# Moving per-head statistics of a recurrent layer's output from VectorE to ScalarE, and reordering the solve around it

## What is computed

```python
_, y = lax.scan(_rwkv7_step, S0, seq)                 # y: tokens x 16 heads x 64
mean = jnp.mean(y, axis=-1, keepdims=True)
var = jnp.mean(jnp.square(y - mean), axis=-1, keepdims=True)
yn = ((y - mean) * lax.rsqrt(var + LNX_EPS)).reshape(B, T, D) * lnx_w + lnx_b
bonus = (jnp.sum(rh * kh * r_k, axis=-1, keepdims=True) * vh).reshape(B, T, D)
out = ((yn + bonus) * g).astype(x.dtype)
return out @ w_o
```

## Time and profile before

| what | us |
|---|---|
| median of three runs | 1098.86 |
| the three runs | 1093.63, 1098.86, 1102.5 |
| the profiled execution, its own time | 1091.18 |
| its span | 1089.3 |

### The profile page before, as it was taken

The page is one execution under the profiler, slowest core; times in us unless marked ns, Lnnn a source line. Parts: engine busy times, 40 slices in busy tenths (PEclk is TensorE's granted clock), DMA queues, the critical chain, the costliest instruction groups (busy, mean ns, idle before and its releaser), DMA issues.

```text
span 1089.3 us, 18693 instructions
## 1 busy us (share of the span) xinstructions
PE 1062.2 (98%) x7143; PEld 917.0 (84%) x7143; DVE 798.9 (73%) x1103; ACT 604.0 (55%) x928; POOL 219.3 (20%) x234
## 2 busy tenths in 40 slices
PE   7999998999999999999999999999999999999997
PEld 6997797888888888789888888998777789888886
DVE  7997878778886658777788756688867776666643
ACT  6766363555564566856666554635665446555532
POOL 0125493121221011002222200571100001122200
PEclk9999999999999999999999999999999999999999
DMA  8553172646666466345667575556452555766552
GB/s 249 172 172 117 39 244 69 175 135 181 187 192 253 167 151 162 121 131 150 187 189 192 194 271 158 159 191 215 154 136 84 194 162 131 193 191 193 193 193 78
DMA packets 219747, 183.11 MB, mean 168 GB/s; under 512 B 43265, under 2 KB 197614, under 8 KB 219678
## 3 DMA queue, kind: packets, MB, share of 16 engines
q1 hardware_dynamic: 215710, 171.43, 52.4%
q0 software_dynamic: 3392, 8.66, 2.5%
q10 hardware_dynamic: 576, 2.07, 0.5%
HBM read 179.44 MB, written 2.69 MB: 167 GB/s over the span
## 4 chain that ended last, share of the span: by engine, by line
PE 80%; DVE 13%; issue 2%; DMA 2%; ACT 1%; POOL 1%; SPq 1%; DVEq 0%; POOLq 0%; ACTq 0%
PE bank L288 20%; PE bank L282 13%; PE bank L284 13%; PE bank L283 13%; PE bank L289 10%; DVE ring L417 3%; PE bank L295 2%; PE bank L1250 2%; DVE arena L1687 1%; DVE arena L1782 1%; DVE stat L1780 1%; PE bank L375 1%; PE bank L2167 1%; DMA arena<-in_kv_w_up 1%; PE bank L1365 1%
## 5 line engine op out<-in xcount | busy, mean ns | idle before, releaser
L417 DVE TENSOR_TENSOR ring<-ring,arena 128x2048 fp32r<-128x2048 f32 (+1 forms) x138 | 312.9, 2271 | 112.4 <-ACT arena L411 110.8
L282 PE MATMUL bank<-arena 128*128 128x512 f32 (+3 forms) x980 | 343.6, 351 | 3.7 <-DVE ring L417 3.0
L288 PE MATMUL bank<-arena 128*128 128x512 f32 x960 | 335.7, 396 | 0.0
L411 ACT ACTIVATE arena<-ring 128x2048 fp32r<-128x2048 f32 (+1 forms) x145 | 272.1, 1879 | 98.0 <-DMA ring<-in_ffn_w_out 42.9
L289 PE MATMUL bank<-arena,ring 128*128 128x256 f32 x960 | 267.2, 278 | 0.0
L284 PE MATMUL bank<-arena 128*128 128x512 f32 (+3 forms) x720 | 264.7, 368 | 0.0
L283 PE MATMUL bank<-ring,arena 128*128 128x512 f32 (+2 forms) x560 | 216.1, 386 | 0.0
L288 PEld LDWEIGHTS bank<-arena 128*128 128x128 f32 x960 | 180.1, 188 | 42.6
L282 PEld LDWEIGHTS bank<-arena 128*128 128x128 f32 x980 | 185.4, 189 | 29.2 <-issue 5.4
L289 PEld LDWEIGHTS bank<-arena,ring 128*128 128x128 f32 x960 | 180.6, 188 | 0.0
L284 PEld LDWEIGHTS bank<-arena 128*128 128x128 f32 x720 | 135.6, 188 | 22.2
(11 more groups left out here) (338 smaller groups left out, 1274.9 us busy)
## 6 DMA issues: line engine op xcount, KB each, us to landing
ring<-in_ffn_w_in SPq DMA_DIRECT2D x80, 512.0 KB, 5.1
ring<-in_ffn_w_out SPq DMA_DIRECT2D x44, 512.0 KB, 4.4
ring<-in_w_gate_up SPq DMA_DIRECT2D x40, 512.0 KB, 5.1
ring<-in_w_in SPq DMA_DIRECT2D x18, 1024.0 KB, 5.1
ring<-in_a_w_rkv SPq DMA_DIRECT2D x12, 1024.0 KB, 5.4
ring<-in_w_down SPq DMA_DIRECT2D x22, 512.0 KB, 3.7
ring<-in_a_w_o SPq DMA_DIRECT2D x4, 1024.0 KB, 6.8
arena<-in_ffn_w_in SPq DMA_DIRECT2D x8, 512.0 KB, 4.7
```

The source lines that it names most:

```text
L282: nc.tensor.matmul(dst, stationary[0], moving[0], start=start, stop=False)
L288: nc.tensor.matmul(dst[:, :], stationary[0], both_parts, start=start, stop=False)
L411: nc.scalar.activation(buf(hi_of(n), 0, w, arena12), ring[:, r, 0:w], ACT.Copy).then_inc(hi_ready, 1)
L417: on.tensor_tensor(ring12[:, r, 0:w], ring[:, r, 0:w], buf(hi_of(n), 0, w, arena12).bitcast(F32), ALU.subtract).then_inc(split_ready, 1)
```

## The change

Seven edits in the lists of four engines:

1. **Statistics on ScalarE.** The 128x32 scaling of the value means, and the four 128x8 scalings of sums to variances, become ScalarE copies with a scale (and a bias). The two sums of values become one over both tiles.
2. **The root's product on ScalarE.** `scaled(a, q)`: eight ScalarE copies of 128x64 out of the bank, each scaled by its head's root, instead of L1811 on VectorE. `gated_out` keeps two instructions.
3. **VectorE's order in the solve.** All block additions of tile 1 come ahead of `gated_out(0, 0)`. The first sum of squares comes ahead of `state_added`.
4. **GpSimd's second centring held** until VectorE's split of the first `w_o` slot is done.
5. **ScalarE's order.** The split of `w_o` slot 1 moves up behind the first squares; `scaled(0, *)` stands ahead of the split of the last `w_o` slot; `scaled(1, *)` behind the early rounded part.
6. **TensorE's order.** Both block inverses of tile 1 ahead of `o_turn(0, 0)`; `o_turn(1, 1)` ahead of (1, 0).
7. **VectorE's order behind the solve.** Both last `w_o` splits ahead of `gated_out(1, *)`. `early_lo(0, 0)` moves from between `o_lo(1, 0)` and `o_lo(1, 1)` to the place of `early_lo(0, 1)`, and that one behind `turn_dve` of tile 0.

```diff
 # ffn_front_dve
             x_scaled(dve, i + 1, 0, xn)
             if f != 1:
-                early_lo(dve, f, 1)
-            turn_dve(dve, turn, 0, 4, hi, lo)
+                early_lo(dve, f, 0 if f == 0 else 1)
+            turn_dve(dve, turn, 0, 4, hi, lo)
+            if f == 0:
+                early_lo(dve, f, 1)
             post_scale(dve, i, 1)
 # rwkv_pe
             block_inverses(1, 0)
+            block_inverses(1, 1)
             o_turn(0, 0)
-            block_inverses(1, 1)
             for q in range(2):
-                pe.wait_ge(u_out, 2 + q + 1)
+                pe.wait_ge(solve_out, 4 + q + 1)
                 y_solved(1, q)
...
                 elif (a, s) == (1, 0):
+                    o_turn(1, 1)
                     pe.wait_ge(o_split, 3)
-                elif (a, s) == (1, 1):
-                    o_turn(1, 1)
 # rwkv_act
             def squares(a, q):
                 act.wait_ge(ymm, 2 * a + q + 1)
-                if a == 1:
-                    act.wait_ge(var_ready, 2 + q + 1)
+            def variance(a, q):
+                stat = slice(a * H + 8 * q, a * H + 8 * (q + 1))
+                act.wait_ge(stats_ready, 2 + 2 * a + q + 1)
+                nc.scalar.activation(y_var[:, stat], y_sq[:, stat], ACT.Copy, bias=LNX_EPS, scale=1.0 / N).then_inc(var_ready, 1)
+            def scaled(a, q):
+                act.wait_ge(rstd_ready, 2 + 2 * a + q + 1)
+                for h in range(8 * q, 8 * q + 8):
+                    op = nc.scalar.activation(toks(W_YC)[:, a, h * N:(h + 1) * N], bank[Y_BANK[a][q]][:, h % 8 * N:(h % 8 + 1) * N],
+                                              ACT.Copy, scale=y_rstd[:, a * H + h:a * H + h + 1])
+                op.then_inc(solve_out, 1)
...
+            act.wait_ge(stats_ready, 1)
+            nc.scalar.activation(v_mean, v_sum, ACT.Copy, scale=-1.0 / N).then_inc(stats_ready, 1)
             for b in range(4):
                 step_evac(b)
...
             squares(0, 0)
+            act.wait_ge(state_mm, 1)
+            ahead(act, FIRST["w_o"] + 1, split_act)
+            variance(0, 0)
             squares(0, 1)
+            variance(0, 1)
             ahead(act, FIRST["w_o"] + 2, split_act)
+            scaled(0, 0)
+            scaled(0, 1)
             act.wait_ge(sweep_mm, SOLVED + SWEEP_NO[1, 2])
             ahead(act, LAST["w_o"], split_act)
             solutions(1, 0)
             solutions(1, 1)
             o_evac(0, 0)
             squares(1, 0)
+            squares(1, 1)
             o_evac(0, 1)
-            squares(1, 1)
+            variance(1, 0)
+            variance(1, 1)
             early_hi(act, 0, 0)
+            scaled(1, 0)
+            scaled(1, 1)
             o_evac(1, 0)
             o_evac(1, 1)
 # rwkv_dve
-                nc.vector.tensor_scalar(y_var[:, stat], y_sq[:, stat], 1.0 / N, LNX_EPS, ALU.mult, ALU.add).then_inc(var_ready, 1)
...
-                dve.wait_ge(rstd_ready, 2 + 2 * a + q + 1)
-                link(dve, nc.vector.tensor_tensor(by_head(yc), by_head(bank[Y_BANK[a][q]][:, :]), spread(y_rstd[:, stat].unsqueeze(2), [P, 8, N]), ALU.mult))
+                dve.wait_ge(solve_out, 4 * a + 2 + q + 1)
...
-            for a in range(NT):
-                value_means(a)
+            nc.vector.tensor_reduce(v_sum, by_head(buf(W_V)), AX, ALU.add).then_inc(stats_ready, 1)
...
+            squares_summed(0, 0)
             state_added(0)
             state_added(1)
-            variance(0, 0)
+            squares_summed(0, 1)
             block_added(1, 0, 1)
-            variance(0, 1)
             block_added(1, 0, 2)
             block_added(1, 1, 1)
-            gated_out(0, 0)
             block_added(1, 0, 3)
             block_added(1, 1, 2)
             block_added(1, 1, 3)
+            gated_out(0, 0)
             gated_out(0, 1)
             o_lo(0, 0)
             ahead(dve, FIRST["w_o"] + 1, split_dve)
-            variance(1, 0)
+            squares_summed(1, 0)
             o_lo(0, 1)
-            variance(1, 1)
+            squares_summed(1, 1)
             ahead(dve, FIRST["w_o"] + 2, split_dve)
+            ahead(dve, LAST["w_o"], split_dve)
             gated_out(1, 0)
-            ahead(dve, LAST["w_o"], split_dve)
             gated_out(1, 1)
             o_lo(1, 0)
-            early_lo(dve, 0, 0)
             o_lo(1, 1)
 # rwkv_pool
             rest_gated(0)
+            pool.wait_ge(split_ready, SPLIT_NO[FIRST["w_o"]] + 1)
             values_centred(1)
             rest_gated(1)
```

More of the change, by code:

```diff
@@ L1118, in build @@
         (n_saved, nd_landed, solved, y_saved, z_zeroed, z_landed, cleared, tok_mm, tok_evac, u_mm, u_rhs, step_mm, step_in,
-         sweep_mm, sum_ready, u_out, rem_mm, state_mm, state_ready, ymm, lnx_landed, means_ready, s1_zeroed, c_ready,
+         sweep_mm, sum_ready, solve_out, rem_mm, state_mm, state_ready, ymm, lnx_landed, stats_ready, s1_zeroed, c_ready,
          o_ready, o_mm, o_in, o_split) = (
             sem(n) for n in ("n_saved", "nd_landed", "solved", "y_saved", "z_zeroed", "z_landed", "cleared", "tok_mm",
-                             "tok_evac", "u_mm", "u_rhs", "step_mm", "step_in", "sweep_mm", "sum_ready", "u_out", "rem_mm",
-                             "state_mm", "state_ready", "y_mm", "lnx_landed", "means_ready", "s1_zeroed", "c_ready",
+                             "tok_evac", "u_mm", "u_rhs", "step_mm", "step_in", "sweep_mm", "sum_ready", "solve_out", "rem_mm",
+                             "state_mm", "state_ready", "y_mm", "lnx_landed", "stats_ready", "s1_zeroed", "c_ready",
                              "o_ready", "o_mm", "o_in", "o_split"))
         xs_hi, xs_split, low_mm = sem("xs_hi"), sem("xs_split"), sem("low_mm")
-        early_mm, early_evacuated = rem_mm, u_out
-        EARLY_MM0, EARLY_OUT0 = (2, 8, 15), 4
+        early_mm, early_evacuated = rem_mm, solve_out
+        EARLY_MM0, EARLY_OUT0 = (2, 8, 15), 8
         EARLY_SPLIT0 = [XS_SPLIT["v"] + n for n in (0, 7, 11)]
@@ L1448, in rwkv_pe @@
                 if h % 8 == 0:
-                    pe.wait_ge(u_out, h // 8 + 1)
+                    pe.wait_ge(solve_out, h // 8 + 1)
                 lo, c, hv = (h % 2) * N, h // 2, slice(h * N, (h + 1) * N)
@@ L1638, in solutions @@
                 act.wait_ge(sweep_mm, SOLVED * a + SWEEP_NO[g, NB])
-                nc.scalar.activation(u[a][:, g * HALF:(g + 1) * HALF], bank[(0, 4)[a] + g][:, :], ACT.Copy).then_inc(u_out, 1)
+                nc.scalar.activation(u[a][:, g * HALF:(g + 1) * HALF], bank[(0, 4)[a] + g][:, :], ACT.Copy).then_inc(solve_out, 1)
             def squares(a, q):
                 act.wait_ge(ymm, 2 * a + q + 1)
-                if a == 1:
-                    act.wait_ge(var_ready, 2 + q + 1)
                 nc.scalar.activation(y_squared[q], bank[Y_BANK[a][q]][:, :], ACT.Square).then_inc(squared, 1)
+            def variance(a, q):
[8 more added lines that the diff above has]
+                op.then_inc(solve_out, 1)
             def o_evac(a, q):
@@ L1799, in at_bank, with squares_summed @@
                 return toks(W_YC)[:, a, q * HALF:(q + 1) * HALF], slice(a * H + 8 * q, a * H + 8 * (q + 1))
-            def variance(a, q):
+            def squares_summed(a, q):
                 stat = at_bank(a, q)[1]
                 dve.wait_ge(squared, 2 + 2 * a + q + 1)
-                link(dve, nc.vector.tensor_reduce(y_sq[:, stat], by_head(y_squared[q]), AX, ALU.add))
-                nc.vector.tensor_scalar(y_var[:, stat], y_sq[:, stat], 1.0 / N, LNX_EPS, ALU.mult, ALU.add).then_inc(var_ready, 1)
+                nc.vector.tensor_reduce(y_sq[:, stat], by_head(y_squared[q]), AX, ALU.add).then_inc(stats_ready, 1)
             def gated_out(a, q):
@@ L1836, in block_added @@
                 nc.vector.tensor_tensor(rhs[a][rows, cells], bank[g][rows, :], rhs[a][rows, cells], ALU.add).then_inc(sum_ready, 1)
[L1838 to L1841, removed]
             def state_added(g):
@@ L1929, in values_centred @@
             def values_centred(a):
-                pool.wait_ge(means_ready, a + 1)
+                pool.wait_ge(stats_ready, 2)
                 pool.wait_ge(u_mm, 2 * (a + 1))
```

## The result

The changed kernel takes 1088.14 us (median of four, 1085.78 to 1089.63) against 1100.3 us (median of four, 1093.63 to 1102.5) for the kernel before, taken beside it.

A forecast was written before the change was run, and what follows sets the result against it. TensorE was taken as the bound, busy 1062.2 of 1089.3 us. Gains reaching 4.6 us at tile 0's transposition, less a new gap of 1.5 at tile 1's, left 3.0: 1098.86 less 3.0, 1095.9 us; range 1089 to 1102.

The forecast's parts named there:

- Value means: Sums and scalings of the value means: TensorE waits for nothing there, GpSimd starts about 1 us later; costed at 0.
- Centring held: First `w_o` split on VectorE takes 2.28 instead of 3.53 us, TensorE's 0.63 gap goes: 0.6 us gained.
- First block addition: Tile 1's first block addition no longer stands behind a stalled scaling; TensorE's 1.31 gap shrinks to 0.1: 1.2 us gained.
- the additions ahead: Only two additions stand between tile 1's sweeps, ahead of `gated_out(0, 0)`; a 0.4 gap is left: 0.4 us gained.
- ScalarE's products: `scaled` at 0.25 us a product: TensorE waits 0.5 for the first solution, 0.8 us given back, projection starts at 175.1.
- Turn moved up: Last turn ahead of (1, 0): the 1.99 gap ahead of tile 0's transposition goes whole, 4.6 us gained at this mark.
- Early remainders: Two of 2.28 us each delay tile 1's norm: new gap of 1.5 ahead of its transposition, 3.0 us left.
- A gain lost again by the end: Sign of being wrong: a gain at tile 1's transposition that is lost again by the end of the span.
- ScalarE as the pace: Rival: scaled products cost more than 0.25 us; gain used up at 0.375, 1101.2 us at 0.47; chance 0.08.
- The held root: Rival: GpSimd's last root can't get in between the two last `w_o` splits; gain 2.2, 1096.7 us; chance 0.20.
- The stalls: Rival: VectorE's long split and long scaling have another cause than GpSimd, or move; gain about 1, 1097.9 us; chance 0.10.
- the second remainder: Rival: the second early remainder holds tile 1's norm less than reckoned; the full 4.6 stays, 1094.3 us; chance 0.12.

The follow-up runs named there:

- experiment 8: The changed kernel without GpSimd's wait ahead of the second centring: 1087.61 us, ratio 0.9885 to before.
- experiment 2: The changed kernel again, unaltered: 1089.01 us, ratio 0.9901 to before.
- experiment 1: The kernel before again, unaltered, under another name: 1100.89 us, ratio 1.0001.
- the halves: Two kernels: the change without its moved last turn and early remainders, 1091.02 us (ratio 0.9929), and the kernel before with only those moves, 1094.8 us (0.9947).
- the tail alone: The kernel before with only the last turn moved ahead of (1, 0) and the early remainders in their new places: 1094.8 us, ratio 0.9947.
- Experiment 3: The changed kernel with the last turn and both early remainders left in their old places: 1091.02 us, ratio 0.9929 to before.
- experiment 10: The changed kernel with early remainders back in their old places, plus twelve filler products in TensorE's wait ahead of the second pair products: 1083.5 us, ratio 0.9878.

## Why the prediction was wrong

The median moved four times as far as forecast. By the prediction's own steps:

- **Value means, costed at 0.** This is the step that failed. "TensorE waits for nothing there" was read from one execution, in which it was true. What I missed stood in that profile: the 1.18 us of a scaling that takes 0.17 when alone, next to a GpSimd operation, with a 4.5 us one queued right behind. I had named the mechanism for two other places and not looked for it here, and bounded the cost by what one execution showed. Measured: 6.2 us alone, 6 to 7 when taken back, 7.5 when only the masking is held. The 0.03 that I gave to a gain above 11 us rested on the same step: I measured the room by the idle time of that one execution.
- **The time of one execution taken as the kernel's.** I noted that the profiled execution lay 7.7 below the median and moved on. That gap was the clue: the other executions did something else. Taking the same 3.0 off the median assumed that they did not.
- **Centring held, 0.6.** The split's time came out as forecast (2.28), and so did its worth: 0.7 at the last sweep (13.05 us against 13.79 in experiment 8).
- **First block addition, 1.2, and the additions ahead, 0.4.** Forecast last sweep at 168.2, found at 168.37, idle 0.33 ahead of it (0.41 in experiment 2) against a forecast of 0.4.
- **ScalarE's products.** Forecast 0.25 each, found 0.2; the wait of 0.5 for the first solution did not come, and the projection started at 174.7, not 175.1.
- **Turn moved up.** The 1.99 gap went whole; transposition at 195.35, forecast 196.2.
- **Early remainders.** The new gap came as forecast in place, 0.90 instead of 1.5. Tile 1's transposition stood at 206.23 against 207.6. So the part that I had priced gave 4.4 us at this mark where 3.0 were forecast. That the profiled execution then came out at 1088.07 against 1088.2 is luck: behind the mark it took 1.4 us longer than before (880.1 against 878.7). A gain lost again by the end was a sign of being wrong that I had named; since two executions of the changed kernel differ by 3.0 there, it can't be put down to the change.
- **What the rest is.** Tile 1's transposition stands at 219.47 in experiment 1, a typical execution of before, and at 206.23 in the changed kernel: 13.2 us, for spans that are 12.5 apart. Of these, 7.2 are the lost race, 1.6 are low clock between the two transpositions, and 4.4 are the part that I had priced. How often each occurs in the runs that were not profiled stays open, and with it how the 12 us of the medians divide and why the halves overlap; the gain of 6.1 for the tail alone belongs there (its profile, an execution that lost the race, shows only some 3 of it: 216.11 at the mark). The low clock comes and goes: in four of six profiles with the gap of 2.0 us ahead of tile 0's transposition the clock fell behind it, and the two transpositions lay 11.4 to 11.5 us apart instead of 9.9. Experiment 3's timeline:

```profile
197.35 1.78 PE L375 MATMUL bank<-cst,arena 128*128 128x128 f32 x8 [1.98 <-DVE arena L566]
...
208.78 1.08 PE L375 MATMUL bank<-cst,arena 128*128 128x128 f32 x8
```

None of the eight profiles without that gap has this stretch.

- **The rivals.** ScalarE as the pace is out: its price is below the forecast's. The held root did not show either: the two last roots took 4.57 us together, so the second got in between the two splits. Nor were the splits held by a root: the two took 4.49 us together from 177.61, with the first root running since 176.82. The stalls did not stay, and the second remainder was not covered (0.90 idle). The range reached down to 1089, as I took the 9 us scatter of before for scatter that both kernels share, where a large part is the race won or lost: the changed kernel's first four runs spread over 3.9 us.

## What to carry to other kernels

Look up every tiny VectorE or GpSimd operation that takes several times its usual duration beside an operation of the other engine, and ask what that other engine has queued right behind: here the price was not what the first execution showed but what stood queued behind it, and moving the tiny operation to ScalarE, or holding the long one by a wait on it, each cured it. When the profiled execution lies outside the spread of the timed ones, profile again before costing anything at nothing. Compare marks inside the traces and not spans alone: here the untouched 880 us behind the last mark scattered by 3 us for one kernel. After moving work, look where the engine that got free now idles, and put what you displaced there.

## What the runs showed of the hardware

- A VectorE operation that GpSimd already holds up is not sure to run next. The scaling, issued at 137.75 while GpSimd's operation ran until 139.18, was held by GpSimd's next one as well, issued at 139.13; so it went in four of five profiles in which nothing prevented it. By their times most executions of before went the same way. The Trainium skill, SBUF — State Buffer, section "SBUF: two separate sides", has it that whichever starts first keeps the port for the whole instruction. The trace agrees in that the short scaling (1.18 and 1.15 us) ends with the centring; it does not for GpSimd's roots, beside which splits ran at their usual 2.28. In the four long ones (6.79 to 7.21 us) the row ends 0.03 behind a memset, the third GpSimd operation in a row; the loss to operations issued later is this case's.
- Of thirteen profiles with a wait of 1.8 to 1.9 us near 125 us, seven kept the clock behind it and six fell to half speed for 3 to 4 us (the expectation of experiment 10 miscounts them); the 48 products behind it then took 7.8 to 8.1 us instead of 6.4. The same list of instructions did both (6.44 and 8.10 in two profiles of the changed kernel), so two profiles can differ by up to 1.7 us at that place; between the first two of before and after the difference was gone by 154.8. With the wait filled (experiment 10) the clock stayed up in the one profile taken.
- ScalarE's 128x64 products out of PSUM with a per-partition scale are issued 0.20 us apart (sixteen in 3.39), those from SBUF 0.24 apart (eight in 2.01); the single durations, 0.29 to 0.38, say nothing of that.
